# A two-block sequence model on one core: prologue of attention C for two heads together, narrow projections in one tile, and other orders of work in GLA, the merge and attention A

## What is computed

```python
# first block: one input projection, four branches, a gated merge, then an FFN
proj = rmsnorm(x) @ w_in      # ... dt (8 columns), gla_low_rank (16 columns), merge gates (4 x 1024)
log_a = log_sigmoid(gla_low_rank @ gla_gate_w + gla_gate_b) / 16     # decay of GLA
ys = [hgrn2(...), ssd(..., dt), gla(..., log_a), rglru(...)]         # each 1024 x 512
merged = sum_n sigmoid(merge_gate[n]) * (ys[n] @ w_branch[n])
h = x + merged @ w_out;  h = h + ffn(h);  x = rmsnorm(h)
# second block, even layer: A = windowed attention (8 heads, 64 wide) with a bias, B = axial RoPE
oa = neighbourhood_attention(rmsnorm(qa), rmsnorm(ka), va, rpb)
x = x + (concat(oa, ob) * silu(gate)) @ w_out_e
# odd layer: C has low-rank queries and keys, 64 + 32 wide a head, the 32 rotated and shared by the keys
q = rmsnorm(cq) @ w_cq_b;  k_nope, v = split(rmsnorm(ckv) @ w_ckv_b)
qc = rotate_last_32(rmsnorm(q));  kc = rotate_last_32(rmsnorm(concat(k_nope, kpe)))
oc = softmax(qc kc^T * 96 ** -0.5) v
# D = difference of two softmaxes a head, 16 of 64 columns rotated
x = x + (concat(oc, od) * silu(gate)) @ w_out_o
```

## Time and profile before

| what | value |
| --- | --- |
| median of 3 runs | 4122.47 us (4120.41 to 4129.11) |
| the profiled execution's own time | 4110.4 us |
| its span, first to last instruction | 4108.5 us |
| mean granted TensorE clock | 0.966 of full speed |
| TensorE busy | 3800.1 us (92%) |
| VectorE busy | 1831.6 us (45%) |
| ScalarE busy | 1297.3 us (32%) |
| GpSimd busy | 910.3 us (22%) |

### The profile page before, as it was taken

One profiled execution on the slowest core, in us unless ns is written; L12 is line 12 of the kernel. 1 busy time (PEld: TensorE's weight loads), 2 busy tenths in 40 slices (PEclk: granted clock), 3 DMA queues, 4 the chain that ended last, 5 costly groups with the idle time before them and its releaser, 6 DMA issues.

```text
span 4108.5 us, 51728 instructions
## 1 busy us (share of the span) xinstructions
PE 3800.1 (92%) x21728; PEld 2981.4 (73%) x21728; DVE 1831.6 (45%) x2276; ACT 1297.3 (32%) x1521; POOL 910.3 (22%) x560
## 2 busy tenths in 40 slices
PE   6999999989999999999999899999887999988888
PEld 5778887867777778888887676666675566766667
DVE  5364444633715631101104555555652556445562
ACT  3243332332411011001002333445522566434341
POOL 3212221222323433333332311100031001101001
PEclk8999999999999999999999999999998999999999
DMA  3111111111135421111113111100021001100011
GB/s 131 36 42 52 52 42 42 42 52 44 47 112 163 131 72 51 51 46 49 49 45 130 55 41 40 37 14 29 32 79 29 12 12 25 34 19 24 16 52 65
DMA packets 276747, 215.07 MB, mean 52 GB/s; under 512 B 16240, under 2 KB 254992, under 8 KB 276528
## 3 DMA queue, kind: packets, MB, share of 16 engines
q1 hardware_dynamic: 256656, 146.01, 12.6%
q10 hardware_dynamic: 19872, 65.94, 4.5%
HBM read 170.11 MB, written 37.75 MB: 51 GB/s over the span
## 4 chain that ended last, share of the span: by engine, by line
PE 78%; DVE 11%; ACT 6%; issue 3%; ACTq 1%; DMA 0%; SPq 0%; DVEq 0%; POOL 0%; POOLq 0%
PE ps L329 32%; PE ps L346 16%; PE ps L377 12%; DVE AR L2062 3%; PE ps L1068 2%; DVE SM L2742 2%; DVE AR L2070 2%; PE ps L591 2%; PE ps L311 2%; PE ps L1079 1%; PE ps L1059 1%; PE ps L288 1%; PE ps L1090 1%; PE ps L422 1%; PE ps L404 1%
## 5 line engine op out<-in xcount | busy, mean ns | idle before, releaser
L2868 POOL CAST WH<-WR 128x1024 fp32r<-128x1024 f32 (+2 forms) x270 | 277.1, 1026 | 3048.4 <-DMA WR<-in_w_in 849.6
L2870 POOL TENSOR_TENSOR WL<-WR,WH 128x1024 fp32r<-128x1024 f32 (+2 forms) x270 | 594.5, 2202 | 21.6
L329 PE MATMUL ps<-XH,WH 128*128 128x512 f32 (+1 forms) x1984 | 503.3, 396 | 16.3 <-DVE AR L2336 9.6
L329 PE MATMUL ps<-XH,WL 128*128 128x512 f32 (+1 forms) x1984 | 491.1, 390 | 0.0
L329 PE MATMUL ps<-XL,WH 128*128 128x512 f32 (+1 forms) x1984 | 490.0, 389 | 0.0
L329 PEld LDWEIGHTS ps<-XH,WH 128*128 128x128 f32 (+1 forms) x1984 | 367.0, 187 | 104.0 <-DVE AR L2336 10.0
L2062 DVE TENSOR_TENSOR AR<-AR 128x512 f32<-128x512 f32 (+2 forms) x345 | 393.6, 1141 | 88.1 <-ACT AR L1538 39.4
L329 PEld LDWEIGHTS ps<-XH,WL 128*128 128x128 f32 (+1 forms) x1984 | 369.0, 186 | 82.7
L329 PEld LDWEIGHTS ps<-XL,WH 128*128 128x128 f32 (+1 forms) x1984 | 368.0, 185 | 81.8
L346 PE MATMUL ps<-ARR,WH 128*128 128x512 f32 x1600 | 398.8, 391 | 16.4 <-ACT ARR L1622 8.6
L346 PEld LDWEIGHTS ps<-ARR,WH 128*128 128x128 f32 x1600 | 301.3, 188 | 82.8 <-issue 10.0
(11 more groups left out here) (241 smaller groups left out, 5147.3 us busy)
## 6 DMA issues: line engine op xcount, KB each, us to landing
WR<-in_w_in SPq DMA_DIRECT2D x78, 512.0 KB, 3.8
WR<-in_w_ffn_in SPq DMA_DIRECT2D x44, 512.0 KB, 3.8
spill<-H ACTq DMA_DIRECT2D x32, 512.0 KB, 2.7
gates<-AR ACTq DMA_DIRECT2D x32, 512.0 KB, 2.8
AR<-gates SPq DMA_DIRECT2D x32, 512.0 KB, 3.5
H<-spill ACTq DMA_DIRECT2D x32, 512.0 KB, 5.3
WR<-in_w_in_e SPq DMA_DIRECT2D x26, 512.0 KB, 3.8
WR<-in_w_in_o SPq DMA_DIRECT2D x23, 512.0 KB, 3.9
```

The source lines that it names most:

```text
L329: mm = pe.matmul(pt[0:m, h * 512:h * 512 + 512], wp[:, slot, k, 0:m], xp[:, k, h * 512:h * 512 + 512], start=i == 0, stop=i == 3 * KD - 1)
L2868: pool.tensor_copy(hi, full).then_inc(s_whi, 1)
L2870: pool.tensor_tensor(lo, full, hi, ALU.subtract).then_inc(s_wsplit, 1)
```

## The change

It has six parts. (a) `prep_c0` does the work of prep_c(0) and prep_c(1) as well, the two heads side by side, with the gates gc0 and gc1 between the steps; prep_c makes a gate only for pairs 2 and 3. (b) In `raw` the square comes before the rotation's DMAs. (c) dt and the GLA low-rank input are one job of m=48, whose weight is loaded by two DMAs, one after the other; ScalarE copies the 16 rows out, writes them to HBM and loads them back to A(11) at u = 3; a merge gate stands where `glr` was, so the last row of gates has ten. (d) gz(5), its log decay and its sums move into the second half of u = 4. (e) The roundings of the first two branches come between gate stores, from the 23rd on; VectorE's wait for all gate stores moves to b = 1; on SP each weight load of the merge goes ahead of the gate load before it. (f) In attention A VectorE yields twice a step, after the output's multiply and after the probabilities, and `prep_a` and `prep_b0` are placed anew. The lines stand up to twelve columns further left than in the file.

```diff
@@ -447,7 +449,7 @@
     xgemm(("sx", f), cols(win, SX + f * P))
-xgemm(("dt",), cols(win, SDT, 8), m=8)
+xgemm(("dt",), (cols(win, SDT, 32), cols(win, GLR, 16)), m=48)
@@ -550,17 +552,21 @@
+def gz(u):
+    gemm(("gz", u), a["gla_gate_w"][0][:, (u - 4) * P:(u - 3) * P], rhs=lambda k: A(11), kp=16, nk=1)
...
     if u == 4:
-        xgemm(("glr",), cols(win, GLR, 16), m=16)
+        mg()
...
         w = u - 4
-        pe.wait_ge(freed[bank(("glr",))], turn(("glr",)))
-        gemm(("gz", u), a["gla_gate_w"][0][:, w * P:w * P + P], rhs=lambda k: A(11), kp=16, nk=1)
+        if u == 4:
+            pe.wait_ge(s_low_in, 16)
+            gz(4)
@@ -673,6 +679,7 @@
         elif u == 4:
+            gz(5)
@@ -762,10 +769,12 @@
     for i in range(KD):
-        loads.append(("gate", 8 * b + i))
...
                    branch if i == 0 else None)
+        if b or i:
+            loads.append(("gate", 8 * b + i - 1))
+loads.append(("gate", 31))
@@ -863,17 +872,17 @@
     yield
+    hn(("ka", p), "w64", [A(22)])
...
     yield
-    hn(("ka", p), "w64", [A(22)])
+    KREADY.append(hb(2))
...
     yield
-    KREADY.append(hb(2))
@@ -935,11 +944,33 @@
     xgemm(("kpe",), cols(wio, OKPE, 32), m=32)
-    hb()
+    low_q = hb()
     hn(("ckv",), "w128", [A(16)])
-    last = hb()
-    pe.wait_ge(freed[bank(last)], turn(last))
-    yield
+    xgemm(("gc", 0), cols(wio, OG))
+    pe.wait_ge(freed[bank(low_q)], turn(low_q))
+    for h in range(2):
+        gemm(("qc", h), cols(wcq, h * 96, 96, nk=2), rhs=lambda k: A(18 + k), m=96, nk=2)
+    low_kv = hb()
+    xgemm(("gc", 1), cols(wio, OG + P))
+    hq(("qc", 0), "w96", 96)
+    hq(("qc", 1), "w96", 96, A(24))
+    pe.wait_ge(freed[bank(low_kv)], turn(low_kv))
+    for h in range(2):
+        gemm(("kc", h), cols(wckv, h * 128, 64, nk=1), rhs=lambda k: A(28), m=64, nk=1)
+    values_c(0)
+    for h in range(2):
+        hn(("kc", h), "w96", [A(16 + h)], 96)
+    pe.wait_ge(freed[bank(("vc", 0))], turn(("vc", 0)))
+    transposes(("vct", 0), A(27))
+    for h in range(2):
+        name = ("hb", cnt["hn"] - 2 + h)
+        spread(name, A(23 + h))
+        CREADY.append(name)
+    yield
...
+def values_c(p):
+    src = wckv.rearrange("k (h c) -> k h c", c=128)[:, 2 * p:2 * p + 2, 64:128]
+    gemm(("vc", p), src, rhs=lambda k: A(28), nk=1)
@@ -949,17 +980,16 @@
     hq(("qc", h), "w96", 96)
-    if h % 2 == 0:
+    if h % 2 == 0 and p >= 2:
...
     yield
-    pe.wait_ge(s_kraw, h + 1)
+    pe.wait_ge(s_kraw, h - 1)
...
     if h % 2 == 0:
-        src = wckv.rearrange("k (h c) -> k h c", c=128)[:, 2 * p:2 * p + 2, 64:128]
-        gemm(("vc", p), src, rhs=lambda k: A(28), nk=1)
+        values_c(p)
@@ -1184,8 +1214,6 @@
 weave(prep_c0(), ())
-weave(prep_c(0), ())
-weave(prep_c(1), ())
@@ -1216,7 +1244,12 @@
     dst = WR[:, w % 4]
-    if len(src.shape) == 2:
+    if isinstance(src, tuple):
+        sp.dma_start(dst[:, :, 0:32], src[0]).then_inc(s_half_in, 16)
+        sp.wait_ge(s_half_in, 16 * (dups[0] + 1))
+        dups[0] += 1
+        src, dst = src[1], dst[:, :, 32:48]
+    elif len(src.shape) == 2:
@@ -1376,9 +1409,11 @@
 act.wait_ge(filled[bank(("dt",))], turn(("dt",)))
-act.activation(A(0)[0:8, :], PS[bank(("dt",))][0:8, :], ACT.Identity, bias=par("dtb", 0, 8))\
-    .then_inc(freed[bank(("dt",))], 1)
+act.activation(A(0)[0:8, :], PS[bank(("dt",))][0:8, :], ACT.Identity, bias=par("dtb", 0, 8)).then_inc(s_act_step, 1)
+act.wait_ge(s_act_step, tick(s_act_step))
+act.activation(A(25)[32:48, :], PS[bank(("dt",))][32:48, :], ACT.Copy).then_inc(freed[bank(("dt",))], 1)
 act.wait_ge(freed[bank(("dt",))], turn(("dt",)))
+act.dma_start(a["gates"][31][0:16, :], A(25)[32:48, :]).then_inc(s_low_out, 16)
@@ -1512,13 +1547,7 @@
 seeds(("yn", 1), A(0))
-for u in range(6):
-    nh = 1 if u < 4 else 2
-    if u == 4:
-        act.wait_ge(filled[bank(("glr",))], turn(("glr",)))
-        act.activation(A(11)[0:16, :], PS[bank(("glr",))][0:16, :], ACT.Copy)\
-            .then_inc(freed[bank(("glr",))], 1)
-        act.wait_ge(freed[bank(("glr",))], turn(("glr",)))
+def decay_log(u):
@@ -1531,6 +1560,16 @@
     act.wait_ge(s_lnr, tick(s_lnr))
...
+for u in range(6):
+    nh = 1 if u < 4 else 2
+    if u == 3:
+        act.wait_ge(s_low_out, 16)
+        act.dma_start(A(11)[0:16, :], a["gates"][31][0:16, :]).then_inc(s_low_in, 16)
+    if u == 4:
+        gate_store(10)
+    if u < 5:
+        decay_log(u)
@@ -1573,6 +1612,8 @@
         act.wait_ge(freed[bank(("o", u, hh))], turn(("o", u, hh)))
+        if u == 4 and hh:
+            decay_log(5)
@@ -1610,17 +1651,24 @@
+def branch_high(b, k):
+    act.activation(R(16 + 4 * (b % 2) + k), A(4 * b + k), ACT.Copy).then_inc(s_yhi, 1)
+    act.wait_ge(s_yhi, tick(s_yhi))
...
+first = [(b, k) for b in range(2) for k in range(4)]
...
     gate_store(27 + gates_at[0] % 2)
+    if first and gates_at[0] > 22:
+        act.wait_ge(s_ys, 16)
+        branch_high(*first.pop(0))
+while first:
+    branch_high(*first.pop(0))
 reload()
-for b in range(4):
+for b in range(2, 4):
+    n = J[("br", b - 2, KD - 1)]
+    act.wait_ge(filled[n % 4], n // 4 + 1)
     for k in range(4):
-        act.wait_ge(s_ys, 16)
-        if b >= 2:
-            n = J[("br", b - 2, KD - 1)]
-            act.wait_ge(filled[n % 4], n // 4 + 1)
-        act.activation(R(16 + 4 * (b % 2) + k), A(4 * b + k), ACT.Copy).then_inc(s_yhi, 1)
-        act.wait_ge(s_yhi, tick(s_yhi))
+        branch_high(b, k)
@@ -1669,19 +1717,19 @@
     act.wait_ge(s_act_step, tick(s_act_step))
+    act.activation(sq[0:m, :], t[0:m, :], ACT.Square)\
+        .then_inc(freed[bank(name)], 1)
+    act.wait_ge(freed[bank(name)], turn(name))
...
         rotated(tmp, dst, starts, half, landed)
-    act.activation(sq[0:m, :], t[0:m, :], ACT.Square)\
-        .then_inc(freed[bank(name)], 1)
-    act.wait_ge(freed[bank(name)], turn(name))
...
-def root(name=None):
...
+def root(name=None, x=A(23)):
...
         cnt["hn"] += 1
-    seeds(name, A(23))
+    seeds(name, x)
@@ -1744,10 +1792,10 @@
     yield
+    root()
...
     yield
-    root()
@@ -1841,10 +1889,40 @@
     root()
+    gate(("gc", 0), A(14))
     act.wait_ge(s_rope_tmp, 6)
+    raw(("qc", 0), A(CQ[0]), A(22), 96, par("gqc", 0, 96), (A(27), (64,), 16, s_rot_in[0]))
+    raw(("qc", 1), A(CQ[1]), A(24), 96, par("gqc", 0, 96), (MSKF, (64,), 16, s_rot_in[1]))
...
     act.wait_ge(s_act_step, tick(s_act_step))
-    yield
+    for h in range(2):
+        shared_key(h, A(16 + h))
+    gate(("gc", 1), A(15))
+    qroot()
+    qroot()
+    for h in range(2):
+        own_key(h, A(16 + h))
+    act.wait_ge(s_rope_tmp, 6 + 1)
+    to_sbuf(("vc", 0))
+    root()
+    root(x=A(24))
+    to_tokens(("vct", 0), A(12))
+    yield
...
+def shared_key(h, square):
+    act.activation(A(CK[h % 4])[64:96, :], A(9)[96:128, :], ACT.Copy).then_inc(s_act_step, 1)
+    act.wait_ge(s_act_step, tick(s_act_step))
+    act.activation(square[64:96, :], A(8)[96:128, :], ACT.Square).then_inc(s_act_step, 1)
+    act.wait_ge(s_act_step, tick(s_act_step))
...
+def own_key(h, square):
+    act.wait_ge(filled[bank(("kc", h))], turn(("kc", h)))
+    t = PS[bank(("kc", h))]
+    act.activation(A(CK[h % 4])[0:64, :], t[0:64, :], ACT.Copy, scale=par("gkc", 0, 64)).then_inc(s_act_step, 1)
+    act.wait_ge(s_act_step, tick(s_act_step))
+    act.activation(square[0:64, :], t[0:64, :], ACT.Square)\
+        .then_inc(freed[bank(("kc", h))], 1)
+    act.wait_ge(freed[bank(("kc", h))], turn(("kc", h)))
@@ -2294,15 +2371,11 @@
 v.wait_ge(s_dve_step, tick(s_dve_step))
-for u in range(6):
-    nh = 1 if u < 4 else 2
-    if u == 4:
-        v.memset(A(12), 0.0).then_inc(s_dve_step, 1)
-        v.wait_ge(s_dve_step, tick(s_dve_step))
+def decay_sums(u):
...
     v.wait_ge(s_dve_step, tick(s_dve_step))
-    if nh == 2:
+    if u >= 4:
@@ -2310,6 +2383,14 @@
         v.wait_ge(s_dve_step, tick(s_dve_step))
...
+for u in range(6):
+    nh = 1 if u < 4 else 2
+    if u == 4:
+        v.memset(A(12), 0.0).then_inc(s_dve_step, 1)
+        v.wait_ge(s_dve_step, tick(s_dve_step))
+    if u < 5:
+        decay_sums(u)
@@ -2389,6 +2470,8 @@
     for hh in range(nh):
+        if u == 4 and hh:
+            decay_sums(5)
@@ -2439,8 +2522,9 @@
 lower_branch(1)
-v.wait_ge(gate_out[1], 16 * 16)
 for b in range(4):
+    if b == 1:
+        v.wait_ge(gate_out[1], 16 * 16)
@@ -2552,19 +2636,17 @@
 def prep_a(p):
-    yield
-    yield
+    yield from pause(5)
...
     hb(A(8 + p % 2), par("gqa"))
-    yield
+    yield from pause(3)
+    hn()
+    yield
+    hb(A(10 + p % 2), par("gka"))
+    yield from pause(2)
     bias(p)
-    yield
-    hn()
-    yield
-    hb(A(10 + p % 2), par("gka"))
-    yield
-    yield
+    yield from pause(4)
@@ -2578,24 +2660,20 @@
-def kb(x, m=P):
-    name = ("hb", cnt["hn"] - 1)
+def kb(x, m=P, name=None):
+    name = name or ("hb", cnt["hn"] - 1)
...
 def prep_b0():
-    yield
-    yield
+    yield from pause(5)
...
     hb(A(6), par("gkb"))
-    yield
+    yield from pause(2)
...
     rope(A(6))
```

(47 more changed lines are left out.)

## The result

The changed kernel takes 4011.03 us (median of 4 runs, 4009.51 to 4015.23), the one before 4121.44 (4 runs, 4118.41 to 4129.11): a ratio of 0.9731, 95% interval 0.9714 to 0.9748, 111 us faster with an uncertainty of 7. Predicted were 4012.5 and a range of 3997 to 4042. The profiled execution took 4010.44.

A forecast was written before the change was run, and what follows sets the result against it. TensorE, busy 3800.1 of 4108.5 us, was taken as the bound in attention C's loop and the merge gates' tail, with idle time elsewhere. Terms summed to -110.7, say -110, from the 4122.5 median: 4012.5 us, range 3997 to 4042.

The forecast's parts named there:

- C's loop: Attention C after its prologue: TensorE bounds it, so losing gate gc1 (10.95) and a little waiting gives -11.5 us (10.9 to 12.4).
- GLA: GLA's last group: with decay work moved into group 4, the gate's 9.59 us bank wait goes; -9 us (-3 to -11).
- D: Squares before rotated DMAs, D and C: L831's 3.1, L1148's 4.3 and a 1.6 cold tail go; -8.7 us (0 to -15).
- Prologue of C: Start of attention C: two heads together remove serial hops, scores start at 64.5 instead of 94.15 us, -29.6.
- rival of a ScalarE chain: Prologue of attention C: the ScalarE-VectorE chain bounds it, L831's 7.1 and a third of L422's 8.3 stay; +10 us, chance 0.10.
- Narrow tile: Narrow projections in one tile: the glr xgemm goes, a merge gate takes its place, the tail has one fewer; -11.1 us.
- rival of the shared port: GLA's decay_sums: each moved VectorE operation meets a GpSimd split, 2.1 us each; +4 us, chance 0.05.
- Merge: Merge start: roundings among gate stores bring the first branch job 12.3 us earlier; SP's weight-load order gives another 1.5.
- Attention A: Attention A: VectorE's split step moves side work into its pause, removing 19 us of waits and 8 of slow matmuls; -27.
- waits that change place: Attention A: if VectorE's step chain is the bound, side work in the pause delays the next negmax; +24 us, chance 0.13.
- L831 in D under 0.5: Sign in attention D: TensorE's waits at source line L831 should fall under 0.5 us.
- The slower rival: Gates before the merge: ScalarE's in-order wait for the RG-LRU result holds gate stores and stops TensorE; 4131 us, chance 0.02.

The follow-up runs named there:

- u_attA: Changed kernel with attention A's orders on TensorE, ScalarE and VectorE, and prep_b0's on VectorE, put back as before: 4045.61 us, ratio 0.9809 to the kernel before.
- u_proC: Changed kernel with attention C's prologue head by head again and gc1 in the loop, the square still ahead of the DMAs: 4048.37 us, ratio 0.9825 to before.

## Why the prediction was right, point by point

The sum was 110.7; the medians differ by 110.4. That they agree so well is partly luck: the first pair of profiles differs by 99.9, and the stages of the two unmodified kernels add up to 102. Against these stages C's loop, GLA, D, and the narrow tile with the merge were priced 2 to 4 us too high each and the prologue 2, and A 6.5 too low, so errors cancelled. The profile that the sum was made against was some 10 us under what that kernel mostly takes; taking the total from the median kept that out of the forecast.

- **Prologue of C, right.** From its sums to the first scores 65.5, predicted 64.5, with VectorE's chain of two rotations and two newtons last, as worked out: 49.8 us up to the second query norm and the first seeds where 48.6 was reckoned, and 15.7 for the chain where 15.9 was. The rival of a ScalarE chain would have kept over 6 of L840's waits; there is none.
- **C's loop, mechanism right, size too high.** gc1's 10.9 went, but the loop gave 8 on the mean. The step that failed is "a stretch that TensorE bounds" taken as free of clock loss and of new waits. Its busy time fell by 9.2, not 10.95, and its idle time rose by 0.9 where 0.5 less was reckoned. Both loops have four waits of 1.5 before the first scores of a pair. In the first profile of before only the first of these four ran slowly (6.01, then 3.67 three times), in that of after the third, behind the same wait; in the other profiles with the part one to four groups of scores took over 4 us. Timelines, before and then after:

```profile
3386.78 3.67 PE L1068 MATMUL ps<-AR 96*128 96x512 f32 x8 [1.55 <-issue]
```

```profile
3283.62 5.37 PE L1098 MATMUL ps<-AR 96*128 96x512 f32 x8 [1.54 <-issue]
```

- **Narrow tile, right**: 11.0 for 11.1, the last ten gates 109.3; its copies, DMAs and the second load cost nothing that shows.
- **GLA, mechanism right, mis-sized**: 4.5 to 6.5 for 9. I had the spread 1.2 late and found 1.86; the term left out is the slow groups behind gz(5), four matmuls with 16 rows: the next two ran in 3.39 and 2.34 against 1.98. That gz(5) is their cause isn't shown, for behind the same four matmuls at 866.23 in the kernel before, and behind gz(4), none ran slowly. No split lay beside decay_sums (its TENSOR_SCALAR took 0.69), so the rival of the shared port did not come up there; it did at the end of the merge.
- **Merge, right in the 12.3** (17.8 to 5.5) and in the 1.5 for the low half (1.47 gone), of which 1.8 came back in front of w_out, a term left out. In two profiles of kernels with the same merge (u_attA and u_proC) it took 180.2 instead of 185.1; in both the last additions took 1.23 each, and that wait was 2.23. Both were run on the same chip and none of the other experiments was, so whether the chip or chance sets how the splits fall is open. The Trainium skill, page "SBUF — State Buffer", section "Who interferes with whom", says that a VectorE operation with two SBUF inputs and a GpSimd one that reads SBUF shut each other out; the trace agrees, with 3.17 for this addition beside a split and 1.22 with none beside it (in u_attA, at 1372.13).
- **Attention A, too small**: 32 for 27. Its price was from the shorter of the two profiles of before; in the first pair of profiles it is 29.6, of which 20.1 are idle time for the 19 reckoned and 9.5 slow matmuls for the 8. The rival, waits that change place, is out: L1058 and L379 on VectorE are at 0.7 together although a pair of probabilities still took 2.15 beside a split (at 2552.86).
- **D, the step that failed**: "L831 waits 3.1 and L1148 4.3 for the square", priced as gain in full. These two were the waits of the first stretch alone; in the whole of D the waits on the square were 13.8, and taking all of them away gave 4, since ScalarE's exponentials were the next late thing, which the prediction had said of the key stages alone. The sign "L831 in D under 0.5" did not come: its line, L840, waited 3.5 for them. The terms named, 3.1, 4.3 and 1.6, also add up to 9.0 and not to 8.7.
- **The slower rival**: ScalarE did wait for the RG-LRU result between gates 22 and 23, 4.16 us where some 5 were reckoned, and no gate waited for a bank (TensorE is busy in all of the 109.30 us of the last gates):

```profile
1138.11 1.06 ACT L1655 ACTIVATE ARR<-AR 128x1024 fp32r<-128x1024 f32 x1 [4.16 <-DVE AR L2137]
1139.20 1.03 ACT L1454 ACTIVATE AR<-ps 128x1024 f32<-128x1024 f32 x1
```

## What to carry to other kernels

Put work of the engine that bounds the stage (here whole gates of 11 us) into each hop of a serial chain, and side work of an engine into the time in which it waits anyway, one operation for each pause that is long enough for one. A wait on an engine that is busy up to the next need of it, as ScalarE in D, is worth only what that engine's next late result leaves: ask for each wait taken away what would have come last without it. And price a stage from more than one profile where it holds many short waits.

## What was not expected

The same instructions run for different times from one execution to the next, and it is the stages with short waits that do it. The eight matmuls of C's first scores, with 1.5 us idle before them every time, took 3.67 in one execution of the changed kernel and 6.9 in the next; TensorE's granted clock was 0.50 of full (1.2 of 2.4 GHz) for 2 us from 3285.5 in the first of these, behind a wait of 1.54 that had no such effect in the kernel before. Where most of the waits went, the scatter went too: A, with 10 us of idle time left of 30, took 341.2 to 349.4 in four profiles with its waits, and 311.6 to 312.4 in the nine that have the new order and no other edit there.
